# Seven block products instead of eight in the second FFN's hidden layer, on halves of 256 tokens

## The reference

```python
def swiglu(h, w_in, w_out):
    g, u = jnp.split(h @ w_in, 2, axis=-1)
    return (jax.nn.silu(g) * u) @ w_out
```

## Time and profile before

| | us |
|---|---|
| three runs | 1610.59, 1611.68, 1611.92 |
| median | 1611.68 |
| profiled execution: its own time | 1613.21 |
| profiled execution: span from first to last instruction | 1611.50 |
| TensorE busy with matmuls | 1563.6 |
| VectorE busy | 955.8 |
| ScalarE busy | 669.4 |

### The profile page before, as it was taken

How to read it: one execution, slowest core, us unless ns; L and a number is a source line. 1 busy time by engine, 2 the same in 40 slices (tenths; PEclk the granted TensorE clock), 3 DMA queues, 4 the chain that set the end, 5 groups by cost and what they waited for, 6 DMA issues and landing times.

```text
span 1611.5 us, 23282 instructions
## 1 busy us (share of the span) xinstructions
PE 1563.6 (97%) x9340; PEld 1346.9 (84%) x9340; DVE 955.8 (59%) x1564; ACT 669.4 (42%) x1063; POOL 100.1 (6%) x95
## 2 busy tenths in 40 slices
PE   6999999999999999999999999989999999999998
PEld 4789988888878898989898998867778888888886
DVE  5565536635485565888787757888846533333334
ACT  4325447533364341433342445567744421222222
POOL 0000000000000000000000000046620000000003
PEclk8999999999999999999999999999999999999999
DMA  9341310013233444335333223420002332332332
GB/s 335 101 149 55 112 45 27 27 53 105 80 105 110 153 137 148 108 118 169 109 115 118 81 65 105 113 71 1 2 27 79 105 101 82 104 104 81 103 92 92
DMA packets 197841, 156.46 MB, mean 97 GB/s; under 512 B 7139, under 2 KB 194703, under 8 KB 197743
## 3 DMA queue, kind: packets, MB, share of 16 engines
q1 hardware_dynamic: 197742, 155.10, 31.5%
HBM read 149.84 MB, written 2.10 MB: 94 GB/s over the span
## 4 chain that ended last, share of the span: by engine, by line
PE 80%; DVE 8%; ACT 6%; DMA 3%; issue 2%; SPq 1%; DVEq 0%; ACTq 0%
PE ps L681 77%; DMA w_raw<-in_ffn_w_in 2%; PE ps L1271 1%; DVE w_lo L2025 1%; ACT w_hi L1389 1%; ACT pr L1979 1%; DMA ada_pre<-in_w_ada 1%; DVE scaled L2081 1%; DVE u_acc L2139 1%; PE ps L1276 1%; SPq L476 1%; DVE h_lo L2090 0%; DVE t_sum L2598 0%; DVE t_lo L2603 0%; ACT h_hi L1439 0%
## 5 line engine op out<-in xcount | busy, mean ns | idle before, releaser
L681 PE MATMUL ps<-h_hi,w_lo 128*128 128x512 f32 (+2 forms) x936 | 337.8, 361 | 0.0
L681 PE MATMUL ps<-h_hi,w_hi 128*128 128x512 f32 (+1 forms) x784 | 294.1, 375 | 4.2 <-DVE w_lo L2025 4.0
L681 PE MATMUL ps<-h_lo,w_hi 128*128 128x512 f32 (+1 forms) x784 | 286.6, 366 | 0.0
L2025 DVE TENSOR_TENSOR w_lo<-w_raw,w_hi 128x2048 fp32r<-128x2048 f32 (+1 forms) x57 | 128.5, 2255 | 199.3 <-ACT w_hi L1389 199.3
L681 PEld LDWEIGHTS ps<-h_hi,w_lo 128*128 128x128 f32 x936 | 177.1, 189 | 24.3
L1389 ACT ACTIVATE w_hi<-w_raw 128x2048 fp32r<-128x2048 f32 (+1 forms) x57 | 107.3, 1883 | 197.0 <-DMA w_raw<-in_ffn_w_in 101.4
L681 PE MATMUL ps<-a_hi,w_lo 128*128 128x512 f32 (+1 forms) x528 | 187.0, 354 | 0.0
L681 PEld LDWEIGHTS ps<-h_hi,w_hi 128*128 128x128 f32 x784 | 148.6, 190 | 35.1 <-issue 6.9
L681 PEld LDWEIGHTS ps<-h_lo,w_hi 128*128 128x128 f32 x784 | 148.9, 190 | 24.0
L669 POOL TENSOR_SCALAR pr<-pr,rden 128x384 f32<-128x384 f32 x64 | 82.5, 1296 | 810.5 <-DVE rden L2890 810.2
L681 PE MATMUL ps<-a_hi,out_hi_w 128*128 128x512 f32 (+1 forms) x352 | 121.8, 346 | 2.8 <-DVE a_lo L2579 1.5
(11 more groups left out here) (325 smaller groups left out, 3074.2 us busy)
## 6 DMA issues: line engine op xcount, KB each, us to landing
w_raw<-in_ffn_w_in SPq DMA_DIRECT2D x88, 512.0 KB, 5.1
ada_w<-in_w_ada SPq DMA_DIRECT2D x41, 1024.0 KB, 5.3
w_raw<-in_gla_w_in SPq DMA_DIRECT2D x24, 512.0 KB, 4.8
w_raw<-in_ffn_w_out SPq DMA_DIRECT2D x40, 256.0 KB, 2.9
w_raw<-in_ffn_w_out SPq DMA_DIRECT2D x16, 512.0 KB, 3.9
ada_pre<-in_w_ada SPq DMA_DIRECT2D x7, 1024.0 KB, 11.6
w_raw<-in_gla_w_o SPq DMA_DIRECT2D x8, 512.0 KB, 6.7
w_raw<-in_swa_w_o SPq DMA_DIRECT2D x8, 512.0 KB, 4.6
```

Source lines behind the costliest of these rows:

```text
L681: return pe.matmul(o, w, r, start=start, stop=stop, skip_group_check=skip)
L2025: dve.tensor_tensor(w_lo[s][:, 0:kc, :], raw_of(n)[:, 0:kc, :], hi_of(n)[:, 0:kc, :].bitcast(F32), ALU.subtract).then_inc(wlo_ok, 1)
```

## The change

The second FFN's hidden slabs from the fourth on (74 to 78, 83 to 90, 95 to 100) are done as seven block products as well, with halves of `HT1` = 256 of the 512 latent tokens. The first FFN's helpers get the half length by slab (`half`), the hidden row's place (`a_row`) and its number (`hidden`). The second FFN is written out slab by slab on all engines; the functions `ffn` go. Its parts stay 8, 8 and 6. The output slabs are done as before.

In the opening, ScalarE writes each of the 8 normed chunks a second time to `h1_full`, VectorE forms four sums of quarters (128 x 1024 each) and four low parts, ScalarE four high parts, which go to the context's unused places in `h_hi` and `h_lo`. Slab 74's forms are made while slab 73 is multiplied; its first three high parts have buffers of their own (`form_hi7`).

```diff
+HT1 = LX // 2
+FIRST7 = F1 + 3
+SEVENS0 = len(SEVEN)
...
     def product(n, j):
 
             q, s = SEVEN[n], n % 2
             if j == 0:
                 pe.wait_ge(out_free[s], n // 2)
-            if q == 0 and j in (1, 3, 4, 5):
+            if q in (0, SEVENS0) and j in (1, 3, 4, 5):
 
-                pe.wait_ge(sl_ok, (1, 3, 4, 5).index(j) + 1)
+                pe.wait_ge(sl_ok, (1, 3, 4, 5).index(j) + 1 + 4 * int(q > 0))
...
-            o = bank(slab_banks(n) + (0, 1, 2, 0, 1, 0, 2)[j], 0, HT)
+            o = bank(slab_banks(n) + (0, 1, 2, 0, 1, 0, 2)[j], 0, half(n))
...
-        ffn(1, F1, (LAT,), 1)
+        first_slab(F1, 2, (LAT,))
+        slab(F1 + 1, 0, h_in, (LAT,), k_wait=h_wait(3, 1), joint=True)
+        slab(F1 + 2, 0, h_in, (LAT,))
+        for n in range(FIRST7, N_SLABS):
+            if n in SEVEN:
+                for j in range(7):
+                    product(n, j)
...
@@ ScalarE
+        h1_sum_high(0)
+        h1_sum_high(1)
+        up0(F1 + 1, (LAT,))
+        h1_sum_high(2)
+        high0(F1 + 1, (LAT,))
+        h1_sum_high(3)
+        for j in range(7):
+            form_high(FIRST7, j)
+        up0(F1 + 2, (LAT,))
+        high0(F1 + 2, (LAT,))
+        for n in range(FIRST7, N_SLABS):
+            if n in SEVEN:
+                after = n + 1 in SEVEN
+                head = n - 1 not in SEVEN and n > FIRST7
+                if head:
+                    form_high(n, 3)
+                    form_high(n, 4)
+                part_sum(n, 0)
+                if head:
+                    form_high(n, 5)
+                    form_high(n, 6)
+                if after:
+                    form_high(n + 1, 0)
+                part_sum(n, 1)
+                if after:
+                    form_high(n + 1, 1)
+                gate_one(n)
+                if after:
+                    form_high(n + 1, 2)
+                part_sum(n, 2)
+                if after:
+                    form_high(n + 1, 3)
+                    form_high(n + 1, 4)
+                else:
+                    split(n + 1, 0, OUT1[n + 1][3])
+                part_sum(n, 3)
+                if after:
+                    form_high(n + 1, 5)
+                gate_two(n)
+                if after:
+                    form_high(n + 1, 6)
+                high7(n)
...
@@ VectorE
+        low0(n, LC, T)
+        dve.wait_ge(hf_ok, 2 * DC)
+        h1_sum(0, (1, 1), (1, 0), (1, 1), ALU.add)
+        h1_sum(1, (1, 0), (0, 0), (1, 0), ALU.subtract)
+        h1_sum(2, (0, 0), (1, 1), (0, 0), ALU.subtract)
+        h1_sum(3, (0, 1), (0, 1), (0, 0), ALU.subtract)
+        h1_sum_low(0)
+        h1_sum_low(1)
+        up0(F1 + 1, (LAT,))
+        h1_sum_low(2)
+        low0(F1 + 1, LC, T)
+        h1_sum_low(3)
+        form_sum(FIRST7, 0)
+        form_low(FIRST7, 0)
+        form_sum(FIRST7, 1)
+        form_sum(FIRST7, 2)
+        form_low(FIRST7, 1)
+        form_sum(FIRST7, 3)
+        for j in range(2, 7):
+            form_low(FIRST7, j)
+        up0(F1 + 2, (LAT,))
+        low0(F1 + 2, LC, T)
```

More of the change, by code:

```diff
@@ L562, in _ @@
             load_unit(unit_of(n))
[L564 to L578, removed]
         for n in range(F0, KV0):
@@ L614, in _ @@
             load_slab(n, 0, cols(swa_w_o[0], (n - SO0) * 256))
-        ffn(1, F1)
+        for n in range(F1, N_SLABS):
+            if n in IN1:
+                load_slab(n, 0, gate_up(ffn_w_in[1], IN1[n]))
+            else:
+                part, e, f0, fc = OUT1[n]
+                load_slab(n, 0, cols(ffn_w_out[1], e * 256, fc, f0 * P))
         for t in range(4):
@@ L1117, in _ @@
             unit(unit_of(n))
[L1119 to L1149, removed]
         def product(n, j):
@@ L1363, in square_sums, with ready @@
             return last
-        ffn(1, F1, (LAT,), 1)
+        first_slab(F1, 2, (LAT,))
[5 more added lines that the diff above has]
+                    product(n, j)
+            else:
+                part, e, f0, fc = OUT1[n]
+                done = FC + f0 + fc
+                def ready(k, done=done, fc=fc):
+                    if k in (0, fc - 1):
+                        pe.wait_ge(a_ok, done - (k == 0))
+                last = n == N_SLABS - 1
+                slab(n, 0, a1_in, (LAT,), kc=fc, k_wait=ready, by_chunk=last, between=early_result if last else None)
         pe.wait_ge(ssq_ok, stats_no[0])
@@ L1643, in _ @@
                 raw_high("gla", 0, 2 * (n - GO0) + ch, BOTH)
[L1645 to L1710, removed]
-                        for ch in range(2 - int(l == 1 and e == 3)):
-                            squares(f"ffn{l}", 2 * e + ch, a)
-                        if l == 0:
-                            for ch in range(2):
-                                raw_high("ffn0", KV_EDGE, 2 * e + ch, segs)
-                n += 4
@@ new lines, in _ @@
+        for n in range(FIRST7, N_SLABS):
+            if n in SEVEN:
+                after = n + 1 in SEVEN
+                if n - 1 not in SEVEN and n > FIRST7:
+                    form_low(n, 3)
+                    form_sum(n, 3)
+                    form_low(n, 4)
+                    form_low(n, 5)
+                    form_low(n, 6)
+                if after:
+                    form_sum(n + 1, 0)
+                    form_low(n + 1, 0)
+                gate_sum_one(n)
+                if after:
+                    form_sum(n + 1, 1)
+                    form_sum(n + 1, 2)
+                    form_low(n + 1, 1)
+                    form_low(n + 1, 2)
+                    up_sum_one(n)
+                    form_low(n + 1, 3)
+                    form_sum(n + 1, 3)
+                    up_sum_two(n)
+                    form_low(n + 1, 4)
+                    form_low(n + 1, 5)
+                else:
+                    up_sum_one(n)
+                    split(n + 1, 0, OUT1[n + 1][3])
+                    up_sum_two(n)
+                gate_sum_two(n)
+                if after:
+                    form_low(n + 1, 6)
+                times_gate(n)
+                low0(n, 0, LX)
+            else:
+                part, e, f0, fc = OUT1[n]
+                if e < 3:
+                    split(n + 1, 0, fc)
+                elif part < 2:
+                    form_sum(n + 1, 0)
+                    form_low(n + 1, 0)
+                    form_sum(n + 1, 1)
+                    form_sum(n + 1, 2)
+                    form_low(n + 1, 1)
+                if part < 2:
+                    residual(n, 0, (LAT,), 48 + 40, 2 * e, None)
+                    if e == 3:
+                        form_low(n + 1, 2)
+                elif e < 3:
+                    plain(n, "ffn1", 2 * e, 48 + 40, (LAT,), False)
+                else:
+                    last_pair_out(n)
```

289 lines of the change are left out of this document (145 added, 144 removed).

## The result

| | before | after |
|---|---|---|
| median, us | 1611.8 (4 runs, 1610.59 to 1613.52) | 1636.48 (4 runs, 1635.1 to 1637.15) |
| ratio to before | | 1.0154 (95%: 1.0142 to 1.0166) |
| span of the profiled execution, us | 1611.5 | 1634.6 |
| mean granted clock | 0.990 | 0.989 |

A forecast was written before the change was run, and what follows sets the result against it. TensorE bounded the second FFN; afterwards a 12.0 us loop through load, SiLU and copy would. Opening 9.6, runs 7.9 and 5.6, splits 0.9, clock 2 sum to +26: 1637.7 us, range 1620 to 1648.

The forecast's parts named there:

- TensorE's own work: Second FFN's block slabs: 84 matmuls of 256 columns take 10.08 us per slab, 0.80 less than 10.88.
- Loop 1: Block slabs: slab's end, next load, first sum, SiLU, copy for sixth product, last two products; period 12.0 us against 10.88.
- Loop 2: Block slabs: VectorE's own steps from one slab's first weight sum to the next take 11.26 us per slab.
- Loop 3: Last slab of a run: fourth product's bank waits behind the previous row's high half; ends 17.1 us after its first weight sum.
- the two terms +7.9 and +5.6: Runs of eight and six block slabs: 94.9 us for 87.0 (+7.9) and 70.9 for 65.3 (+5.6).
- The opening: Slabs 73 to 78: second writes and token sums delay the start, TensorE waits 2.8 us at slab 74; +9.6 us.
- The clock: Long waits, priced by one of 2.30 us, may lower TensorE's granted clock: +2 us, between nothing and 5.8.
- rival C: Block slabs: the clock falls in every slab, two products at half speed; 46 us more, 1684 us; chance 0.06.
- D: Block slabs: no change, with loads landing 1.1 us sooner, loop 2 shorter, a period of 10.9; chance 0.03.
- B: Block slabs: VectorE's loop decides, load or copy not in the way; period 11.26, +16, 1628 us; chance 0.14.
- A: Second FFN: TensorE stays the bound, 14.4 us off and 6.3 on for the opening; 1604 us, faster; chance 0.06.
- The unrolled loops: Second FFN written out slab by slab costs nothing; 8 us if the cover for instruction fetching were gone.

The follow-up runs named there:

- e13: The change, with each weight load waiting only for the products still reading its buffer and VectorE's second gate half-row sum ahead of two low halves: 1608.05 us.
- e4: The change with earlier weight loads, ScalarE's sixth-product copy ahead of SiLU and high half, and VectorE's second gate sum ahead of two low halves: 1608.17 us.
- e5: e4 with the block products beginning two hidden slabs later, at slab 76: 1603.22 us.
- e6: e5 with ScalarE's second writes of the first and last normed chunks behind the splits, and one copy in slab 76 ahead of a high half: 1602.46 us.
- e1: The change, with the next slab's loads waiting for the third (gate) and fifth (up) product instead of the slab's end: 1626.08 us.
- e2: The change, with ScalarE's copy for the sixth product ahead of the first SiLU and a high half: 1630.58 us.
- e3: The change, with VectorE's second gate half-row sum ahead of two low halves and the product ahead of another: 1634.68 us.
- e23: The change with ScalarE's sixth-product copy first and VectorE's second gate sum ahead of two low halves, without earlier loads: 1626.06 us.
- e7: The change with nothing edited but the block products beginning two hidden slabs later, at slab 76: 1629.14 us.

## Why the prediction was right, step by step

**TensorE's own work**: 10.08 us per slab was right: it is the period of e13, e4, e5 and e6. The 588 matmuls of e4 in one piece are 0.1205 us each. The Trainium skill's page "TensorE: Matmul & The Clock Gate", section "Back-to-back issue gap", gives an isolated gap that would make it 9.17 per slab, an estimate, and says itself that for short matmuls in a stream with weight loads this gap counts too little. These rows have some 11 ns more per matmul, and they decide.

**Loop 1** was the bound, at 11.9 us against 12.0. The chain shows each of its members. e1 cuts it at the load, e2 at the copy, and both shorten the kernel.

**Loop 2** was next, at 11.26; e1 shows 11.24. In the change itself VectorE takes 7.22 us from first sum to last half-row sum in slab 74 (7.23 priced).

**Loop 3** at a run's end: the run of eight takes 94.3 us from its first matmul (1378.75) to the first output slab behind it (1473.35), less that slab's wait for the split of 0.28, where 94.9 and 0.45 stood. The run of six takes 69.9 (1517.05 to 1586.96) where 70.9 stood. So by the forecast's own count the two terms +7.9 and +5.6 were +7.3 and +4.6; most of that is the 0.1 to 0.2 us by which each period is shorter. The waits for the splits were 0.28 each, not 0.45.

**The opening**: +9.6 was +10.8 (1335.10 less the wait of 0.28, plus 1.26, against 1325.29, where the first output slab starts before the change):

```profile
1325.29 0.39 PE L681 MATMUL ps<-a_hi,w_hi 128*128 128x512 f32 x1
```

Its points fell close: slab 73 at 1259.63 (1259.7 expected, shifted), the wait of 2.71 (2.8), the end of the wait for the first copy at 1280.61 (1280.59). The 1.2 more is one load that took 6.45 us (from 1311.28, the weights of slab 78) where the others took some 5.3. It is not the chance of one execution: in the traces of e2, e3 and e23 the load of this slab took 6.76, 6.75 and 6.57. In that of e7 it took 5.17. What makes it slow was not tried.

**The clock** is the step that failed. I charged +2 for a lower clock behind the long waits of the opening; the trace shows none. The stretches from 1264 to 1284, length, busy by engine, clock, DMA share, GB/s:

```profile
1264.00:1270.00 6.00, 6.00 (x29) 4.95 (x28) 5.97 (x6) 3.18 (x5) 0.00 (x0) 1.00 0.00 0
1270.00:1276.00 6.00, 2.95 (x20) 2.34 (x19) 5.90 (x10) 3.72 (x6) 0.00 (x0) 1.00 0.64 175
1276.00:1280.00 4.00, 2.61 (x22) 2.41 (x21) 3.58 (x6) 2.02 (x4) 0.00 (x0) 1.00 0.02 4
...
1380.00:1470.00 90.00, 81.79 (x639) 77.52 (x639) 71.67 (x127) 49.23 (x106) 0.00 (x0) 1.00 0.34 94
```

The granted clock stays 1.00, the level of 2.4 GHz, through a stretch in which TensorE was busy 2.95 of 6 us, and in the run (last line) with its waits in every slab. So rival C is out too. I had taken the one wait nearest in length as a price, 2.30 us in the attention; length alone was not what counted. That wait did not stand alone: TensorE was busy 1.70 us of the 4 from 1056 to 1060 and waited again right behind it:

```profile
1062.39 1.22 PE L681 MATMUL ps<-k_st,q_st 128*128 128x256 f32 x4 [1.64 <-ACT pr L1979]
```

Whether that is what tells the two places apart no run here shows. Neither the wait of 2.71 us nor 40 short ones brought the clock down. The Trainium skill's section "HAM oscillation — how this bites in real kernels" of the same page has its case from a kernel with longer waits for data than any of these, so these waits neither bear it out nor speak against it.

**A term that was not there**: TensorE waits 0.93 us at 1604.44 for a split of the last run's output slabs. It is a slow load again: 5.33 us for a slab of 1536 columns, and the split starts 5.78 us after the end of the slab that freed its buffer (1595.32 to 1601.10). In the kernel before it was about 4.4 (1573.5 to 1577.94). The change does not touch these slabs. In the traces of e2, e3 and e23 the same wait is 0.32 to 0.37, in those of the other six kernels there is none; why was not tried.

**The sum**: read in both traces from the first matmul of a stage to that of the next, the difference is 11.1 in the opening, 7.4 in the run of eight (94.60 against 87.23), 4.2 in the run of six (69.91 against 65.75), 0.3 in the two blocks of output slabs between and 1.4 behind the last run: 24.4 with the waits for the splits. The spans differ by 23.1, and with the 1.26 of the earlier start by 24.4. The forecast had, counted the same way, 10.0, 8.4, 5.6, nothing, nothing, and 2 for the clock. So +26 was near in part by luck: the clock's 2 us did not come and the runs were overpriced by 2.4, but the opening's slow load added 1.2 and the last output slabs, with a slow load of 0.9 in them, 1.4. **D**, no change, fell with the waits. **B** is e1. **A** is e13 and e4: I had said that it wants 1.9 us off loop 1 and 1.2 off loop 2, and the two edits of e13, neither of which reaches 1620 alone, do just that.

The unrolled loops cost nothing that shows: in e4 588 matmuls follow each other in one piece.

## What to carry to other kernels

Before you give an engine less work, write down every loop that comes back from one tile to the next, through each buffer's load and through each engine's fixed order, and price it; the new period is the longest of them, not the work. Here TensorE's work fell from 10.88 to 10.08, but a loop through a load, a SiLU and a copy took 11.9. When two loops are both above the work, cutting one shows only the way down to the next (10.4 us for the load, 1.8 at most for VectorE's order), and both together show all (28.4): a small result of one edit is no reason to drop it.

## What was unexpected of the hardware

The clock: a wait of 2.71 us, with TensorE busy for half of the 6 us around it, left the granted clock at 1.00, while 2.30 us in the attention had been followed by 0.62 and 0.53. In the attention a second wait of 1.64 us came right behind the first. What tells the two places apart was not tried.

Loads of the same size (a hidden slab, two of 512 KB) took from 5.03 to 6.45 us within one execution of the change, and that of slab 78 took over 6.4 in the traces of four kernels (the change, e2, e3, e23); where a loop goes through a load, such a slow one is on the path in full.
